# A two-layer hybrid decoder on one core: the scan's angles, the first powers of B and the second powers of C in other slots

## The reference: what is computed

```
a = exp((lam_re + i lam_im) * dt)              # one complex number a state
x_t = B u_t          (B scaled by (a-1)/lam)
h_t = a h_{t-1} + x_t                          # associative_scan over 256 tokens
y_t = Re(C h_t) + d * u_t
```

## Time and profile before

| | |
|---|---|
| median of 3 runs | 952.5 us |
| the profiled execution, and its span | 952.75 us, 951.0 us |
| TensorE busy | 936.0 us (98%) |
| VectorE, ScalarE, GpSimd busy | 610.0, 575.4, 111.3 us |
| in 193 to 254 us (one step): PE, DVE, ACT busy of 61.0 us | 59.24, 54.35, 47.51 us |

### The profile page before, as it was taken

The page is one execution under the profiler, slowest core; times in us unless marked ns, Lnnn a source line. Parts: engine busy times, 40 slices in busy tenths (PEclk is TensorE's granted clock), DMA queues, the critical chain, the costliest instruction groups (busy, mean ns, idle before and its releaser), DMA issues.

```text
span 951.0 us, 15769 instructions
## 1 busy us (share of the span) xinstructions
PE 936.0 (98%) x5939; PEld 796.3 (84%) x5939; DVE 610.0 (64%) x971; ACT 575.4 (60%) x928; POOL 111.3 (12%) x126
## 2 busy tenths in 40 slices
PE   7999999999999999999999999999999999999998
PEld 7998888778878999888888788888888888888886
DVE  4688889799797954855644555555555555555553
ACT  4689886876967746544545573555456545554332
POOL 3101002011020000000002540220021002200000
PEclk9999999999999999999999999999999999999999
DMA  8776544445343467555999986668999866654662
GB/s 285 185 190 196 156 133 134 136 135 175 112 140 127 137 198 266 179 192 190 175 166 180 195 239 169 182 174 160 171 160 172 197 175 178 176 175 156 212 213 85
DMA packets 116007, 165.83 MB, mean 174 GB/s; under 512 B 19301, under 2 KB 56298, under 8 KB 115690
## 3 DMA queue, kind: packets, MB, share of 16 engines
q1 hardware_dynamic: 99504, 159.67, 64.0%
q10 hardware_dynamic: 16442, 5.33, 2.3%
HBM read 162.86 MB, written 2.11 MB: 173 GB/s over the span
## 4 chain that ended last, share of the span: by engine, by line
PE 82%; ACT 7%; DVE 6%; issue 3%; DMA 1%; POOL 1%; ACTq 0%; SPq 0%; DVEq 0%
PE bank L456 21%; PE bank L458 21%; PE bank L457 21%; PE bank L483 3%; PE bank L484 3%; PE bank L485 3%; ACT wh L969 2%; ACT res L1078 2%; PE bank L600 1%; ACT res L1090 1%; DVE wl L977 1%; ACT scr L1230 1%; DVE scr L1747 1%; PE bank L592 1%; DMA res<-in_x 1%
## 5 line engine op out<-in xcount | busy, mean ns | idle before, releaser
L977 DVE TENSOR_TENSOR wl<-raw,wh 128x1024 fp32r<-128x1024 f32 x295 | 362.0, 1231 | 252.7 <-ACT wh L969 251.5
L969 ACT ACTIVATE wh<-raw 128x1024 fp32r<-128x1024 f32 x295 | 310.5, 1058 | 190.2 <-PE bank L458 119.5
L456 PE MATMUL bank<-wh,xh 128*128 128x512 f32 x768 | 307.1, 400 | 0.3 <-DVE wl L977 0.3
L458 PE MATMUL bank<-wh,xl 128*128 128x512 f32 x768 | 300.0, 391 | 0.0
L457 PE MATMUL bank<-wl,xh 128*128 128x512 f32 x768 | 299.2, 390 | 0.0
L458 PEld LDWEIGHTS bank<-wh,xl 128*128 128x128 f32 x768 | 144.1, 188 | 31.1
L456 PEld LDWEIGHTS bank<-wh,xh 128*128 128x128 f32 x768 | 144.3, 188 | 29.0 <-DVE wl L977 0.7
L457 PEld LDWEIGHTS bank<-wl,xh 128*128 128x128 f32 x768 | 144.5, 188 | 27.7
L456 PE MATMUL bank<-wh,yh 128*128 128x512 f32 x256 | 100.5, 393 | 0.0
L458 PE MATMUL bank<-wh,yl 128*128 128x512 f32 x256 | 99.7, 390 | 0.0
L457 PE MATMUL bank<-wl,yh 128*128 128x512 f32 x256 | 99.6, 389 | 0.0
(11 more groups left out here) (317 smaller groups left out, 1022.4 us busy)
## 6 DMA issues: line engine op xcount, KB each, us to landing
raw<-in_o_w_in SPq DMA_DIRECT2D x128, 512.0 KB
raw<-in_e_w_in SPq DMA_DIRECT2D x130, 256.0 KB, 3.3
raw<-in_e_w_out SPq DMA_DIRECT2D x32, 512.0 KB
raw<-in_o_w_out SPq DMA_DIRECT2D x32, 512.0 KB
raw<-in_e_w_in SPq DMA_DIRECT2D x31, 512.0 KB
raw<-in_s_w_glu SPq DMA_DIRECT2D x8, 512.0 KB
res<-in_x SPq DMA_DIRECT2D x8, 256.0 KB, 6.8
res<-in_x SPq DMA_DIRECT2D x1, 2048.0 KB, 9.6
```

The source lines that it names most:

```text
L456: nc.tensor.matmul(o, l_hi, w_hi, start=first, stop=False)
L458: mm = nc.tensor.matmul(o, l_lo, w_hi, start=False, stop=last)
L969: nc.scalar.activation(wh[:, j % RING, :], raw[:, j % RING, :], ACT.Copy).then_inc(hi_done, 1)
L977: nc.vector.tensor_tensor(wl[:, j % RING, :], raw[:, j % RING, :], wh[:, j % RING, :].bitcast(F32), ALU.subtract).then_inc(lo_done, 1)
```

## The change

Four numbers of the slot tables change. The scan's angles go from slot 0 (both parts) to slots -2 and -1, which are slots 14 and 15 of the step before; ScalarE's table, which is in the slot after the second part, goes with them from slot 1 to slot 0. The second `s5_far` goes from slot -4 to -5, and the first `s5_powers` from -10 to -8. No instruction is added or removed. TensorE's, GpSimd's and SyncE's own order stays as it is.

```diff
-TAB_SLOT, FAR_SLOT, BA_SLOT = [0, 0], [-7, -4], [-10, -4]
+TAB_SLOT, FAR_SLOT, BA_SLOT = [-2, -1], [-7, -5], [-8, -4]
```

## The result

The changed kernel takes 980.42 us (median of 4 runs, 978.77 to 980.72), the kernel before 952.49 in the same comparison: a ratio of 1.0294, 95% interval 1.0276 to 1.0312. The forecast was 978.1, range 968 to 986. The profiled execution took 980.72 us, 27.97 more than that of the kernel before.

A forecast was written before the change was run, and what follows sets the result against it. TensorE, busy 98%, was taken as the bound, with tight pace on all three engines. 4.6 + 6.85 + 5.88 + 5.88 = 23.2 us gave 975.7; 2.4 for the clock made 978.1 us, range 968 to 986.

The forecast's parts named there:

- The angles and the table: ScalarE's table, now ahead of the copies of turns 1 to 3, waits for VectorE's angles; L696 6.9 us later.
- the signs: Expected in the trace: L1054 waiting 4 to 5 us for L1657, L666 near 6 us three times, L696 67.4 us apart.
- The loop: TensorE's lateness delays VectorE's next stretch, so each step between L696 grows by 5.88 us to 67.39, the first by 6.85.
- Rival A: ScalarE regains the whole 3.2 us in slot 1, step 65.2 us, total 969.2 us; chance 0.14.
- The first batch: VectorE's wait ahead of slot 15's split is filled by the angles; L696 at 120.49 instead of 115.91, 4.6 us later.
- The other two edits: Moved powers of B and C: L564's 1.23 us wait goes, 1.1 to 2.4 us comes in slot 12; net 0.
- The clock: TensorE at half clock behind two of its three long waits at turn 3, 1.2 us each, 2.4 us.
- The sum: Later L696 of the four batches, 23.2 us, gives 975.7 us without the clock; with 2.4 us for the clock, 978.1.
- rival B: TensorE's clock falls at every wait at turn 3, 2.5 us each: 985.7 us; chance 0.12.
- C: Rival: faster, angles ready by 228.7, so the table fills a ScalarE pause and L564's waits go: 949.8 us; chance 0.03.
- D: Rival: the order changes but turn 3 isn't really held, so time stays within 0.2%; chance 0.03.

The follow-up runs named there:

- e5: Changed kernel, with TensorE kept busy by transposes of the identity during its wait ahead of turn 3: 974.85 us, 951.80 for the kernel before.
- e2: Kernel before with only the angles and the table moved, powers of B and C as before: 978.34 us, 952.25 for the kernel before.
- e1: Changed kernel with the angles back in slot 0 and the table in slot 1, other two edits kept: 957.43 us, 952.25 for the kernel before.
- e3: Changed kernel with ScalarE's table back in slot 1, angles left in slots -2 and -1: 956.74 us, 952.25 for the kernel before.
- e6: Changed kernel with both parts of the angles in slot -3 and the table in slot 0: 960.89 us, 951.80 for the kernel before.
- e4: Changed kernel with the angles back in slot 0 and the table left in slot 0: 987.53 us, 952.25 for the kernel before.

## Why the prediction was right, step by step

**The angles and the table: right.** `tab_ang` to the next L696 was put at 9.24 us; with the clock up (e5) it measures 9.24. The table took 3.09 us to the start of the copies (249.23 to 252.32), 0.1 less than was put in. The row has the Abs end at 249.86, the load start at 249.88 and the Sin start at 251.18, 1.30 us behind the load's start, so the drain of the Trainium skill, ScalarE: Activation LUTs, section What ACT_TABLE_LOAD costs, doesn't show here either. Of the signs, ScalarE's first wait was 2.6 us and not 4 to 5, the long stands were 5.4 us and not near 6 (both not followed up), and L696 came at 122.4, 190.9, 259.3 and 327.8 us for 120.5, 188, 255 and 322, of which more below.

**The loop: right.** L696 to `rotate_out` and on to `tab_ang` was put at 17.27 + 40.88 = 58.15 us. It is 249.12 - 190.92 = 58.20, of it 40.87 gapless on VectorE. A round was to last 67.39 and lasts 67.45 without the clock. Rival A, a round of 65.2, fell by the reason given against it: ScalarE's near copies of slot 2 wait for TensorE's block (L681), at 267.41 again for 2.21 us.

**The first batch: off by 1.9 us.** It was put at 4.6 and is 6.47. Two terms were missing: 0.9 us are the clock, which was to stay up behind a stand of 3 us and didn't; and the changed execution was later before any moved instruction came. VectorE's split in slot 4, before and after:

```profile
76.49 1.22 DVE L977 TENSOR_TENSOR wl<-raw,wh 128x1024 fp32r<-128x1024 f32 x1
```

```profile
77.71 1.22 DVE L977 TENSOR_TENSOR wl<-raw,wh 128x1024 fp32r<-128x1024 f32 x1
```

These 1.2 us are the start of the two executions, which differs as told with e2. 4.6 + 0.9 + 1.2 = 6.7: the estimate was 0.2 too high.

**The other two edits: right.** L564's wait gone, L511's 5.5 us in its place, and both without effect beside the stand; without the moved table they cost 5 us (e1).

**The clock: right in kind, mis-sized in count.** The step as put was "I take 1.2 at two of the three long stands, 2.4 us". It fell at all four stands: the granted clock is 0.50, 1.2 GHz, from 184.43 to 187.84 and 1.00, 2.4 GHz, from 188.5 on, after TensorE had stood 5.39 us; the first fall came with a stand of 2.96 us:

```profile
116.06 0.66 PE L666 MATMUL bank<-con,scr 128*128 128x128 f32 x4 [2.96 <-ACT scr L1065]
```

Each cost about 1.0 us (a round of 68.47 against 67.45), 4.0 in all against the 2.4 that I had taken. For the three long stands the trace agrees with the Trainium skill, TensorE: Matmul & The Clock Gate, section HAM oscillation (a fall each time), and not with the two falls that I took; the fall at the shorter first stand is what the trace alone shows.

That one fall came out near the 1.2 us is partly luck, for two of its parts were wrong and cancel. Turn 3 took 0.5 us longer, as put. The near block took 2.24 us (254.00 to 256.24) against 1.25 at full clock in e5: 1.0 more, where 0.4 was put. The slot's matmuls hardly slowed, 0.1 us, where 1.0 was put: the granted clock had fallen within the stand already, and in this batch the matmuls are back at 0.39 us from the second on.

**The sum.** The forecast of 978.1 was 2.3 us low. Without the clock it was 975.95 for the profiled execution; e5's took 974.12, and 975.5 with its start evened to that of the kernel before: 0.5 too high. With 4.0 for the clock and 1.2 for the late start it is 980.7, the 980.72 that were measured. The measured median lies above all that the forecast itself allowed for (975.7 to 979.3, up to three falls) and below rival B; the count of falls is what it had wrong.

**The rivals.** B (a fall at every stand, 2.5 us each) had the count right and the price two and a half times too high. C and D didn't occur; e3 and e6 show that what decides is when the angles are ready for the table, as C said: with the table back behind the copies, or the angles 4 us sooner, the loss is down to 4.5 and 9 us. Of these, 5 us are the other two edits (e1).

## What to carry to other kernels

When a producer is moved ahead in a schedule and its consumer goes with it by rule, look at when the producer will be ready, not at its slot: here VectorE's angles were 4.4 us behind ScalarE, and a wait that had stood behind the urgent copies came to stand ahead of them. A lateness that returns to its own cause is paid once a round, so find the shortest way round (here L696, near block, `rotate_out`, angles, table, L696) and add it up; that sum was right to 0.1 us. A wait ahead of a longer one for something else costs nothing as long as the longer one is there (e2 against the changed kernel), and its whole length once that is gone (e1). And work that nobody waits for is to stand behind the work that another engine waits for, or where its own engine waits anyway: the moves of B, `hold`, padding and C together gave 947.55 us against 952.04, though not each of them could be told alone.

## What the runs showed of the hardware

- Behind a stand of 2.96 us the clock was halved (in the first batch the near block and the first matmuls; turn 3, at 0.66 us, was not slowed yet). In a stand of 5.39 us the granted clock fell within the stand: it reads 0.57 over 181.00 to 184.40. In e6, with stands of up to 1.0 us at turn 3, it stayed up, and so it did in e5 with 0.4 us.
- The price isn't in proportion to the stand: behind 5.4 us each round lost 1.0 us, behind 6.73 us (e2) 1.0 to 1.2, and behind 6.5 us (e4) 2.3, 1.1 and 2.1. Filling the stands of the changed kernel with transposes that nobody needs kept the clock at 1.00 and gave its 4.0 us back (e5).
